# Finer handovers at the first weight units, unread products on TensorE before the memory has landed, and other banks and another order in the second attention

## The reference

```python
def memory_cross_attention(h, m, w_q, w_kv, q_qk_g, k_qk_g, w_o):
    q = rms_norm((h @ w_q).reshape(B, S, CROSS_HEADS, CROSS_HEAD_DIM), q_qk_g)
    kv = m @ w_kv
    k = rms_norm(kv[..., :D_MODEL].reshape(B, M, CROSS_HEADS, CROSS_HEAD_DIM), k_qk_g)
    v = kv[..., D_MODEL:].reshape(B, M, CROSS_HEADS, CROSS_HEAD_DIM)
    s = jnp.einsum('bshd,bmhd->bhsm', q, k, preferred_element_type=jnp.float32) * (CROSS_HEAD_DIM ** -0.5)
    p = jax.nn.softmax(s, axis=-1).astype(v.dtype)
    o = jnp.einsum('bhsm,bmhd->bshd', p, v).reshape(B, S, D_MODEL)
    return o @ w_o
# in first_block:
        x = x + jnp.concatenate([a_out, r_out], axis=-1) @ w_out[l]
        hc = rms_norm(x, cross_norm_g[l])
        m = rms_norm(mem, mem_norm_g[l])
        x = x + memory_cross_attention(hc, m, cross_w_q[l], cross_w_kv[l], cross_q_qk_g[l],
                                       cross_k_qk_g[l], cross_w_o[l])
```

## Time and profile before

| | |
|---|---|
| median of 3 runs | 964.29 us (962.23 to 964.35) |
| the profiled execution | 962.52 us, its span 960.7 us |
| granted TensorE clock, mean over the span | 0.997 |
| PE busy | 940.7 us (98%), 5036 matmuls |
| DVE, ACT, POOL busy | 742.9, 620.2, 20.5 us |
| chain that ended last | PE 91%, DVE 4%, ACT 2%, issue 1%, DMA 1% |
| HBM read | 213.03 MB, 223 GB/s over the span |

### The profile page before, as it was taken

The page is one execution under the profiler, slowest core; times in us unless marked ns, Lnnn a source line. Parts: engine busy times, 40 slices in busy tenths (PEclk is TensorE's granted clock), DMA queues, the critical chain, the costliest instruction groups (busy, mean ns, idle before and its releaser), DMA issues.

```text
span 960.7 us, 13838 instructions
## 1 busy us (share of the span) xinstructions
PE 940.7 (98%) x5036; PEld 811.6 (84%) x5036; DVE 742.9 (77%) x1102; ACT 620.2 (65%) x940; POOL 20.5 (2%) x40
## 2 busy tenths in 40 slices
PE   7999999999999999999999999999999999999996
PEld 6888888888888888888888899999998888888885
DVE  5567686658799999999999889888896655555575
ACT  6676684656588878878778665747574644434455
POOL 2400000000000000000000000000000000000000
PEclk9999999999999999999999999999999999999998
DMA  9655426425299999999998274836466655555531
GB/s 337 202 176 197 157 89 212 140 87 198 108 367 367 360 349 371 361 359 378 354 367 305 86 223 143 262 110 219 153 217 198 219 175 194 186 188 176 195 111 44
DMA packets 102651, 214.67 MB, mean 223 GB/s; under 512 B 5628, under 2 KB 60176, under 8 KB 96976
## 3 DMA queue, kind: packets, MB, share of 16 engines
q1 hardware_dynamic: 101056, 211.83, 63.2%
q0 software_dynamic: 1392, 2.20, 0.9%
q10 hardware_dynamic: 160, 0.07, 0.0%
HBM read 213.03 MB, written 1.05 MB: 223 GB/s over the span
## 4 chain that ended last, share of the span: by engine, by line
PE 91%; DVE 4%; ACT 2%; issue 1%; DMA 1%; SPq 0%; DVEq 0%; ACTq 0%
PE bank L2155 22%; PE bank L2157 22%; PE bank L2156 22%; PE bank L2814 5%; PE bank L2816 5%; PE bank L2815 5%; PE bank L2160 4%; DMA xs<-in_mem_dram 1%; PE bank L2417 1%; DVE w_lo L449 0%; PE bank L2496 0%; PE bank L2497 0%; PE bank L2399 0%; PE bank L2841 0%; PE bank L2842 0%
## 5 line engine op out<-in xcount | busy, mean ns | idle before, releaser
L2155 PE MATMUL bank<-w_hi,xT_hi 128*128 128x512 f32 (+1 forms) x704 | 280.7, 399 | 0.6 <-DVE xT_lo L1493 0.3
L2157 PE MATMUL bank<-w_hi,xT_lo 128*128 128x512 f32 (+1 forms) x704 | 275.2, 391 | 0.0
L2156 PE MATMUL bank<-w_lo,xT_hi 128*128 128x512 f32 (+1 forms) x704 | 274.8, 390 | 0.0
L2155 PEld LDWEIGHTS bank<-w_hi,xT_hi 128*128 128x128 f32 x704 | 133.3, 189 | 27.2 <-issue 2.2
L2157 PEld LDWEIGHTS bank<-w_hi,xT_lo 128*128 128x128 f32 x704 | 132.5, 188 | 27.6
L2156 PEld LDWEIGHTS bank<-w_lo,xT_hi 128*128 128x128 f32 x704 | 132.8, 189 | 25.3
L447 DVE TENSOR_TENSOR w_lo<-stage,w_hi 128x1024 fp32r<-128x1024 f32 (+3 forms) x99 | 113.6, 1147 | 30.7 <-ACT w_hi L433 29.5
L2814 PE MATMUL bank<-xT_hi,w_hi 128*128 128x256 f32 x440 | 125.0, 284 | 0.4 <-DVE w_lo L449 0.4
L2816 PE MATMUL bank<-xT_hi,w_lo 128*128 128x256 f32 x440 | 124.7, 283 | 0.0
L2815 PE MATMUL bank<-xT_lo,w_hi 128*128 128x256 f32 x440 | 124.7, 283 | 0.0
L433 ACT ACTIVATE w_hi<-stage 128x1024 fp32r<-128x1024 f32 (+3 forms) x100 | 99.6, 996 | 34.2 <-PE bank L2157 14.5
(11 more groups left out here) (424 smaller groups left out, 1374.4 us busy)
## 6 DMA issues: line engine op xcount, KB each, us to landing
stage<-in_w_in_dram SPq DMA_DIRECT2D x36, 1024.0 KB, 5.2
stage<-in_w_gate_up_dram SPq DMA_DIRECT2D x44, 512.0 KB, 4.8
more<-in_expert_w_down_dram SPq DMA_DIRECT2D x17, 1024.0 KB, 6.4
stage<-in_expert_w_gate_dram SPq DMA_DIRECT2D x33, 512.0 KB, 5.2
stage<-in_expert_w_up_dram SPq DMA_DIRECT2D x33, 512.0 KB, 6.4
more<-in_expert_w_gate_dram SPq DMA_DIRECT2D x31, 512.0 KB, 5.1
more<-in_expert_w_up_dram SPq DMA_DIRECT2D x31, 512.0 KB, 6.1
stage<-in_expert_w_down_dram SPq DMA_DIRECT2D x15, 1024.0 KB, 6.7
```

What stands on the lines that cost most here:

```text
L2155: mm(o, k_hi, v_hi, start=start, stop=False)
L2156: mm(o, k_hi, v_lo, start=False, stop=False)
L2157: return mm(o, k_lo, v_hi, start=False, stop=stop)
```

## The change

Six edits. On TensorE: eight unread products ahead of everything and seven between the two halves of the memory's turning; both write bank 3, which nobody reads before its first real product starts it anew. Their operand is a strip of `w_hi` that DVE first sets to 1.0, and PE waits for that (`unread_set`). Unit 1 gets the same finer handover as unit 0. DVE splits unit 6 (`splits_to(7)`) ahead of its wait for the constants and the angles. In the second attention the turning-out of query head 2 goes from DVE to ACT, ahead of the load of the exponential's table; the two halves of unit U_CO+2's split go later on both engines; the waits for turned queries go inside the loop over heads; and the banks are given by hand.

After, the banks are: cs00 4, cs01 7, cs10 7, cp00 4, cp01 6, cs11 5, co00 7, co01 4, cp10 6, cp11 5, catc0 7, catc1 4, co10 6, co11 5, catc2 7, catc3 4. The third scores, cs10, so stand in the bank in which qc1 and then cs01 stood before them.

```diff
-                + ["qc0", "qc1", "cs00", "qc2", "qc3", "cs01", "cs10", "cp00", "cp01", "cs11", "co00", "co01", "cp10", "cp11"]
-                + ["catc0", "catc1", "co10", "co11", "catc2", "catc3", ("moe0", 4), ("moe1", 5), ("router", 6), ("moe2", 4), ("moe3", 7), ("rank", 7)]
+                + ["qc0", "qc1", "cs00", "qc2", "qc3", "cs01", ("cs10", 7), ("cp00", 4), ("cp01", 6), ("cs11", 5), ("co00", 7), ("co01", 4), ("cp10", 6), ("cp11", 5)]
+                + [("catc0", 7), ("catc1", 4), ("co10", 6), ("co11", 5), ("catc2", 7), ("catc3", 4), ("moe0", 4), ("moe1", 5), ("router", 6), ("moe2", 4), ("moe3", 7), ("rank", 7)]
...
         root(head_rstd[:, 0:8], head_inv[:, 0:8], "row_inverse", nth(ROW_ROOTS, "qc")).then_inc(sem("row_rstd"), 1)
+        turned_queries(2)
         warm_up(ACT.Exp)
         cross_exps(0, 0)
-        half_hi(act, U_CO + 2, 0)
         cross_exps(0, 1)
         probs(0, 0)
         cross_exps(1, 0)
         probs(0, 1)
+        half_hi(act, U_CO + 2, 0)
+        cross_exps(1, 1)
         half_hi(act, U_CO + 2, 1)
         split[0] = U_CO + 3
-        cross_exps(1, 1)
         probs(1, 0)
...
+        nc.vector.memset(w_hi[:, RING - 1, 0:640].bitcast(F32), 1.0).then_inc(sem("unread_set"), 1)
         been_read(dve, "mem_gain")
...
-        splits_to(2)
+        dve.wait_ge(main.half_ready, 2)
+        tt(w_lo[:, 1, 0:1024], stage[:, 1, 0:1024], w_hi[:, 1, 0:1024].bitcast(F32), ALU.subtract).then_inc(sem("first_lo"), 1)
+        dve.wait_ge(main.hi_ready, 2)
+        tt(w_lo[:, 1, 1024:SLOT], stage[:, 1, 1024:SLOT], w_hi[:, 1, 1024:SLOT].bitcast(F32), ALU.subtract).then_inc(main.lo_ready, 1)
+        split[0] = 2
...
+        splits_to(7)
         dve.wait_ge(sem("constants_loaded"), 16 * len(small_loads))
...
         cross_top(0, 0)
-        turned_queries(2)
         turned_queries(3)
         cross_top(0, 1)
         cross_top(1, 0)
-        half_lo(dve, U_CO + 2, 0)
         cross_inverse(0)
         cross_top(1, 1)
-        half_lo(dve, U_CO + 2, 1)
-        split[0] = U_CO + 3
+        half_lo(dve, U_CO + 2, 0)
         cross_out(0, 0)
         cross_out(0, 1)
         cross_inverse(1)
         low_parts("catc", None, (0, 1))
+        half_lo(dve, U_CO + 2, 1)
+        split[0] = U_CO + 3
         cross_out(1, 0)
...
-            if u in main.halved:
-                pe.wait_ge(sem("first_lo"), 1)
+            if u < 2:
+                pe.wait_ge(sem("first_lo"), u + 1)
             else:
                 pe.wait_ge(lo_ready, u + 1)
             for k in range(4):
-                if k == 2 and u in main.halved:
+                if k == 2 and u < 2:
                     pe.wait_ge(lo_ready, u + 1)
...
+        def unread(n):
+
+            for _ in range(n):
+                mm(bank[3][:, :], w_hi[:, RING - 1, 512:640], w_hi[:, RING - 1, 0:512], start=True, stop=True)
+
+        pe.wait_ge(sem("unread_set"), 1)
+        unread(8)
         pe.wait_ge(sem("first_loaded"), 16 * len(first_loads))
...
             turn("mem", xs, [(f"mem_loaded{c}", 16)], (2 * c, 2 * c + 1))
+            if c == 0:
+                unread(7)
...
                 h = 2 * p + j
+                been_read(pe, f"qc{h}")
...
-        been_read(pe, "qc0")
-        been_read(pe, "qc1")
         cross_scores(0, 0)
         turn_queries(1)
         cross_scores(0, 1)
-        been_read(pe, "qc2")
-        been_read(pe, "qc3")
         cross_scores(1, 0)
```

## The result

The changed kernel took 965.41 us (median of 20 runs, 963.31 to 967.72), the kernel before 962.59 us (median of 20, 961.95 to 966.05). The ratio of the two is 1.0021, interval 1.0011 to 1.0031: slower by a small but certain amount. The forecast was 963.8 and no difference that can be told. The time lies in the range (962.0 to 965.5), and the change is within 0.3%, but the median went up by 2.8 us where +0.2 was worked out.

What follows compares the result with a forecast made beforehand. PE bounds the kernel, busy 940.7 of 960.7 us. Start -1.6 and second attention +1.8 give +0.2 on the profiled 962.5, so 962.7; the median was put at 963.8, range 962.0 to 965.5.

Steps and rivals of the forecast that it cites:

- The start: First 14 us: unread products raise PE's clock earlier and unit 0 starts sooner; gain 1.2 to 1.9 us, 1.6 taken.
- a margin for a late rise: At the start: if the clock rises only at about 8.8 us, second turns are about 1 us late; 1.6 us taken.
- What is next late: Units 1, 2, 6 after the start: finer handover removes a 0.7 to 0.9 us wait, unit 2 none, early split keeps 1.6.
- The second attention: cs10 in bank 7 must wait for cs01's exponentials; starts 1.8 us later, none won back; bounds -0.2 to +2.3 us.
- rival (a): Second attention: 2.8 us of PE idleness ahead of cs10 lowers the clock, costing 2.3 us; sum +2.5, 966.3 us; chance 0.10.
- the sum: Whole kernel: start -1.6 plus second attention +1.8 gives +0.2 us on the profiled execution, 962.7 us.
- (b): Start: unread products don't lift the clock and delay the turns, unit 0 2 us later; +3.8 us, 967.6; chance 0.06.
- (c): Second attention: third scores are not late, so that part is 0; sum -1.6 to -1.9, 962.1 us; chance 0.12.
- (d): Start gains less than 0.5 us, first half's turns late and clock rising as late as 9; +1.5 us, 965.3; chance 0.10.

Runs made afterwards that it cites:

- eight_only: Kernel before with only the start's edits, without the seven unread products between the two turnings (the eight ahead of everything stay); 960.66 us, one execution.
- attention_alone: Kernel before with only the change's second-attention edits (banks, orders, waits), the start as before; 967.85 us, ratio 1.0037.
- change_again2: The changed kernel unaltered, executed again for a third trace; 967.43 us at a mean granted clock of 0.990.
- router_dense: The change with banks 5 and 7 exchanged, so cs10 follows qc2, and seven instead of three unread wide products at the router; 960.29 us, ratio 0.9965 to before.
- fill_wait: The change with eleven unread products of 512 columns on PE in the wait between cs01 and cs10; 963.91 us, ratio 0.9999 to before.

## Why the prediction was wrong in its direction

**The start** was right in its mechanism and mis-sized: 1.6 was taken, with bounds 1.2 to 1.9. In the profiled run of after it was 2.12, and in the nine traces that have the eight products and both handovers 1.83 to 2.12, so mostly outside the bounds. The memset began at 0.96 and took 0.59 us, so PE began at 1.61 (taken: 1.7):

```profile
0.96 0.59 DVE L1543 MEMSET w_hi<- 128x640 f32 x1 [0.96 <-PEq L2928]
```

In after, unit 0 started at 9.84 and not at 10.05, and its ninth product came 2.00 us earlier than in before. The gain was also put too low because I took off a margin for a late rise. The clock did rise at different moments: in four traces the whole first turning ran at the full clock (1.09 us from 5.4 or 5.5 on), in eight_only none of it. But this hardly reached unit 0: the eleven traces with unread products all start it at 9.70 to 10.09.

**What is next late** was right in all three places, with waits a little shorter than forecast: unit 1 (0.61 us of wait for lack of the finer handover; 0.7 to 0.9 forecast), unit 2 (no wait), unit 6 (1.02 us with the old order; 46.78 against 47.09 - 1.6, so 1.3, by the prediction's numbers).

**The second attention** was right as a wait: cs10 at +1.8 forecast, 1.72 to 1.74 measured (after, its two further traces, attention_alone). The first exponential starts at 193.48, which is 195.60 with the start's 2.12 us added, and 195.59 was forecast. That the bank without the reordering on ACT would have cost another 1.05 us was not tried.

**The step that failed is the argument against rival (a)**, by which the sum has no term for the clock. Rival (a) had 0.10 and a price of 2.3 us once. The argument was that 2.8 us of idleness are less than the 3.5 after which the clock fell at the end of the span. One fall says that 3.5 were enough, not that less is too little. In change_again2 the clock was down after 2.7. The ends of the other traces say the same. Ahead of the fall in the trace of before, PE had been idle for 3.3 us, not 3.5; over the 14 traces that idle time is 2.6 to 4.4 us, and in seven of them below 3.0. The shortest is eight_only, whose last product ends at 950.27 and whose clock falls at 952.9:

```profile
949.88 0.39 PE L2163 MATMUL bank<-w_hi,xT_lo 128*128 128x512 f32 x1
```
```profile
952.00:953.00 1.00, 0.00 (x0) 0.00 (x0) 0.93 (x3) 0.96 (x4) 0.00 (x0) 0.95 0.00 0
953.00:954.00 1.00, 0.00 (x0) 0.00 (x0) 0.75 (x3) 1.00 (x4) 0.00 (x0) 0.50 0.00 0
```

For the change alone it is 2.8 to 3.7 us over three executions. So the same idleness took the clock down sooner or later from execution to execution, and one row of one trace could give no safe length. The price in one place was smaller than thought, 3.64 - 1.99 = 1.65 us on cs10. But it isn't a rare case; together with the router it touched every one of the 29 timed runs that had this wait (20 of after, 9 of attention_alone).

**The second failure was to read the spread of before as noise.** Three runs of 962.2, 964.3 and 964.4 stood there, and I put it down to the rise of the clock at the start. The clock of each run shows it as low stretches, in 28 of 52 executions, and router_dense shows where: at the router. The traced execution was a clean one, so no row of it could show this. The median of before over 20 runs is 962.59, so the forecast also started 1.7 us too high. The sum was made on a clean execution (962.7, and fill_wait's clean runs take 962.3 to 962.6), while the change has no clean run, and its median holds low stretches. That is where the rest lies: the parts of the sum as measured give -2.12 + 1.72 = -0.40, and the median went up by 2.8. That 965.41 still fell into the range is luck, since three errors went against each other: a median of before 1.7 us too high, a gain at the start 0.5 too small, and low stretches left out. (The times of rivals (a) and (b) are 0.2 too high: their sums, which hold the +0.2, were added to 963.8, which holds it too.)

What stays open: why no run of the change is clean, when fill_wait has a third and the kernels without the long wait near a half. Two of three traces of the change sank at the router only, and the two traces that sank behind the wait (change_again2, attention_alone) sank at the router too. If the two falls came independently, each in about half of the executions, some seven of the 29 runs would be clean. None is, so they are most likely linked. That the wait takes down just those executions that the router would otherwise leave alone would fit this, but no trace shows one that sank behind the wait only, and nothing here tests it. Rivals (b), (c) and (d) are refuted by the rows above.

TensorE: Matmul & The Clock Gate of the Trainium skill, section "HAM oscillation — how this bites in real kernels", ties the lower level to idle gaps of PE. The wait for cs10 agrees. At the router the measurement goes further: PE was busy for 3.71 of 4.00 us and had no gap over 0.2 us, but mostly with products of 36 and 72 columns, and the clock sank.

## What to carry to other kernels

When PE must wait or has only narrow products, try wide ones that nobody reads. Here they cost nothing that shows, and at the router they took away low stretches worth up to 4 us in half of the runs. When a bank is reused, count how far down the consumer's chain the reader stands: one place further (cs01's exponentials instead of cs00's) was 1.1 us of PE, and 3 us of the median with what the clock did. Do not take one fall of the clock for the shortest idleness that brings a fall. And read the granted clock of every run before making a sum from one trace: a profile of a clean execution says nothing of what the median holds.

## What the runs showed of the hardware that was not expected

- The clock sank after 2.7 us without a product in one execution of the change, and did not in two others with the same wait. At the end of the span it sank 2.6 to 4.4 us after the end of the last product (14 traces). In attention_alone it sank 0.3 us after PE had taken up work again.
- At the router it sank with PE 93% busy, mostly on narrow products, in nine of 14 traces, and stayed down for 3 to 10 us. The same products did not bring it down in the trace of before. With seven wide products in that stretch instead of three, nine of nine runs are clean.
- The memset of 128 x 640 words took 0.59 us on DVE. VectorE: DVE Perf Modes of the Trainium skill, section "Zero memsets can be issued as uint32 (trn2)", gives one cycle per element, by which 640 columns are an estimated 0.67 us; the measurement decides.
- Eight wide products from 1.61 us on and the first turning were enough for the second turning (9.06) and unit 0 (10.05) to run at the full clock, although the first turning had not and a gap of 1.57 us lay between (eight_only).
